# Four merge-gate half jobs placed inside the prompt attention of a hybrid decoder step, with scores three units ahead and the compressed branch in two halves

## The reference, cut to what matters

```
ng, mg = sigmoid(...)                        # from n @ w_in, w_in[:, 2328:4376] are the merge gates
p_c = softmax(q . kc)                        # compressed branch: at most 32 compressed keys
o = g[..., 0]*(p_c @ vc) + g[..., 1]*o_selected + g[..., 2]*o_window
y = (mg[:, :, 0] * y_conv + mg[:, :, 1] * (o @ w_nsa_out)) @ w_o
x += y;  x += HierMoE(RMSNorm(x));  y_out = RMSNorm_final(x)
```

## Time and profile before

| | |
|---|---|
| runs | 836.99, 840.41, 842.74 us; median 840.41 |
| profiled execution | given by its span of 835.7 us, first to last instruction; the page gives no time around it |
| PE busy | 778.5 us, 93% of the span |
| DVE, ACT, POOL busy | 375.9, 221.1 and 168.2 us |
| chain that ended last | PE 79%, DMA 9%, DVE 6%, issue 3% |
| PE on the chain, gates (L2105) | 15% of the span |
| PE on the chain, attention (L2148, L2123, L2136) | 2% each |

### The profile page before, as it was taken

One profiled execution on the slowest core, in us unless ns is written; L12 is line 12 of the kernel. 1 busy time (PEld: TensorE's weight loads), 2 busy tenths in 40 slices (PEclk: granted clock), 3 DMA queues, 4 the chain that ended last, 5 costly groups with the idle time before them and its releaser, 6 DMA issues.

```text
span 835.7 us, 11541 instructions
## 1 busy us (share of the span) xinstructions
PE 778.5 (93%) x4479; PEld 534.8 (64%) x4479; DVE 375.9 (45%) x799; ACT 221.1 (26%) x480; POOL 168.2 (20%) x270
## 2 busy tenths in 40 slices
PE   5999999997999989999999999999999899998773
PEld 3657778674756657777777777774456755555431
DVE  2201999899778881102006552231237522231106
ACT  2001324152256662233025640000001112221113
POOL 2348447010110006000004520002000212232100
PEclk9999999999999999999999999999999999999979
DMA  9775446130180005152214539703106999999737
GB/s 302 174 17 182 143 101 166 25 122 1 50 292 2 2 2 178 51 176 76 75 51 127 179 89 294 285 1 113 50 26 235 380 374 411 407 403 391 304 137 259
DMA packets 87505, 138.98 MB, mean 166 GB/s; under 512 B 25493, under 2 KB 60465, under 8 KB 86287
## 3 DMA queue, kind: packets, MB, share of 16 engines
q1 hardware_dynamic: 71439, 101.41, 35.5%
q0 software_dynamic: 11392, 32.71, 13.2%
q10 hardware_dynamic: 4616, 4.08, 1.6%
HBM read 132.00 MB, written 21.14 MB: 183 GB/s over the span
## 4 chain that ended last, share of the span: by engine, by line
PE 79%; DMA 9%; DVE 6%; issue 3%; SPq 1%; ACTq 0%; ACT 0%; DVEq 0%; POOLq 0%; POOL 0%
PE ps L1915 18%; PE ps L2105 15%; PE ps L2363 7%; PE ps L2441 6%; PE ps L1939 5%; PE ps L2012 4%; PE ps L2457 3%; DMA mgT<-w_up 2%; PE ps L2148 2%; PE ps L2123 2%; DMA arena<-w_up 2%; PE ps L2136 2%; DMA mgT<-w_in 2%; DMA arena<-yscratch 2%; PE ps L2431 1%
## 5 line engine op out<-in xcount | busy, mean ns | idle before, releaser
L2105 PE MATMUL ps<-xT,keep 128*128 128x288 f32 x512 | 126.9, 407 | 0.8 <-ACT h L1206 0.5
L2105 PEld LDWEIGHTS ps<-xT,keep 128*128 128x128 f32 x512 | 96.5, 190 | 27.4 <-ACT h L1206 0.9
L1915 PE MATMUL ps<-xT,arena 128*128 128x288 f32 x384 | 95.4, 407 | 0.0
L1915 PEld LDWEIGHTS ps<-xT,arena 128*128 128x128 f32 x384 | 72.1, 190 | 19.2
L1395 DVE SCALAR_TENSOR_TENSOR cv<-keep,cv 128x512 f32<-128x512 f32 x120 | 83.7, 748 | 1.4
L2363 PE MATMUL ps<-arena,xT 128*128 128x512 f32 x128 | 55.4, 592 | 0.0
L2441 PE MATMUL ps<-keep,mgT 128*64 128x256 f32 x224 | 41.8, 390 | 4.9 <-DMA mgT<-w_up 3.2
L1939 PE MATMUL ps<-mgT,xT 128*128 128x512 f32 (+1 forms) x128 | 43.5, 498 | 1.2 <-DMA mgT<-w_in 1.2
L2363 PEld LDWEIGHTS ps<-arena,xT 128*128 128x128 f32 x128 | 24.2, 190 | 29.3 <-issue 29.2
L836 ACT ACTIVATE mgT<-ps 64x512 f32<-64x512 f32 x56 | 33.2, 593 | 32.2 <-PE ps L1993 31.6
L1276 ACT ACTIVATE keep<-h 128x1024 f32<-128x1024 f32 (+1 forms) x5 | 5.3, 1059 | 130.1 <-DVE h L1706 121.5
(11 more groups left out here) (412 smaller groups left out, 1340.1 us busy)
## 6 DMA issues: line engine op xcount, KB each, us to landing
arena<-w_down SPq DMA_DIRECT2D x19, 512.0 KB, 16.8
keep<-w_in SPq DMA_DIRECT2D x16, 512.0 KB, 3.8
arena<-w_gate SPq DMA_DIRECT2D x15, 512.0 KB, 8.5
arena<-w_up SPq DMA_DIRECT2D x15, 512.0 KB, 12.5
keep<-w_gate SPq DMA_DIRECT2D x14, 512.0 KB, 10.4
keep<-w_up SPq DMA_DIRECT2D x14, 512.0 KB, 17.6
h<-x_prompt SPq DMA_DIRECT2D x8, 512.0 KB, 5.4
arena<-w_in SPq DMA_DIRECT2D x8, 512.0 KB, 7.5
```

The source lines that it names most:

```text
L1915: last = mm(tokens(j)[:, b, :], weights(k), halves(x[:, k, :])[:, b, :], start=k == 0, stop=k == n_k - 1)
L2105: last = mm(out[:, 0:half], wmg[n // 2 % 3][:, k, :], xT[:, k, (n % 2) * half:(n % 2 + 1) * half], start=k == 0, stop=k == KD - 1, skip_gr ...
```

## The change

- `GATES_IN = 4`: half jobs 0 to 3 of the gates go into the attention, in slot 3: half job 0 in `obank` before the first value products, half jobs 1 to 3 in `cbank`, whole or in pieces of one or two of their eight matmuls behind the value products of units 0 to 5, 12 to 17 and 19 to 23. ScalarE copies them into `mgT` without the sigmoid, which it does for the four at once after the attention.
- TensorE's order in a unit becomes `turns(u)`, `scores(u + 3)`, `values(u - 1)`, then a piece of a gate.
- The compressed branch runs for two head groups at a time: scores of 512 columns instead of 256, softmax passes twice as wide and half as many, transposes onto 128 partitions, `PcT` on all partitions, `vcB` held twice.
- The eighteen empty transposes are left out; half job 0 stands there.
- The third place of the weight ring moves to `keep3`. Tiles 0 and 1 are issued when the taps of the convolution are done, tiles 2 and 3 after the last rotated query; tiles 4 and 5 after the attention.
- After the attention, half jobs 4 to 7 stand where 0 to 3 stood, 8 to 11 where 4 to 7 stood, 12 and 13 where 8 and 9 stood, and 14 to 21 where 10 to 21 stood.

```diff
+GATES_IN = 4
+ORDER += mg_jobs(0, GATES_IN)
-ORDER += [("keys", 0, 0), ("keys", 0, 1)] + mg_jobs(0, 4) + ["mean"] + mg_jobs(4, 8) + [("keys", 0, 2)] + mg_jobs(8, 10) + ["var"] + mg_jobs(10, 22)
+ORDER += [("keys", 0, 0), ("keys", 0, 1)] + mg_jobs(GATES_IN, 8) + ["mean"] + mg_jobs(8, 12) + [("keys", 0, 2)] + mg_jobs(12, 14) + ["var"] + mg_jobs(14, 22)
...
-        wmg = [cut(1024 * s, KD, P, base=k2) for s in range(3)]
+        wmg = [cut(1024 * s, KD, P, base=k2) for s in range(2)] + [cut(2080, KD, P, base=k3)]
...
+        gate_pieces = [(0, 2), (2, 4), (4, 5), (5, 6), (6, 7), (7, 8)]
+        gates_behind = {u: (1, *gate_pieces[u]) for u in range(PER_C)}
+        gates_behind.update({2 * PER_C + n: (2, *gate_pieces[n]) for n in range(PER_C)})
+        gates_behind.update({3 * PER_C + 1 + n: (3, *x) for n, x in enumerate([(0, 2), (2, 4), (4, 5), (5, 6), (6, 8)])})
+        C_SCORES, C_LESS, C_NORM, C_TURNS = PER_C + 1, PER_C + 2, PER_C + 3, 2 * PER_C - 1
...
 # SyncE
-            conv_done(sp)
+            for c in range(CC):
+                sp.wait_ge(s_tap[c], TAPS)
             take(sp, JOB["cso"])
-            for n in range(3):
+            for n in range(2):
                 mg_weights(n)
+            result_of(sp, JOB["rope", HPG - 1])
+            mg_weights(2)
+            mg_weights(3)
             sp.wait_ge(s_kvout, 16 * N_KVOUT)
             sp.wait_ge(s_pv, NU)
             keys_window(0)
             values_window(0)
-            for n in range(3, 6):
+            for n in range(4, 6):
                 mg_weights(n)
             keys_window(1)
             sp.dma_start(wco, a["w_conv_out"][0].rearrange("(c p) n -> p c n", p=P)).then_inc(s_wo, 16)
             for n in range(6, 2 * KD):
                 mg_weights(n)
...
 # ScalarE, after the attention
             keys_turned(0, 0)
-            merge_gates(*range(4))
+            result_of(act, JOB["mg", GATES_IN - 1])
+            nc.scalar.activation(mgT[:, 0:GATES_IN // 2, :], mgT[:, 0:GATES_IN // 2, :], ACT.Sigmoid)
+            merge_gates(*range(GATES_IN, 8))
...
 # VectorE, in the attention
-                if u % PER_C == 2 and u // PER_C + 1 < HPG:
-                    cmp_maxima(u // PER_C + 1)
                 probs_turned(u)
-                if u % PER_C == 4 and u // PER_C + 1 < HPG:
-                    cmp_normalize(u // PER_C + 1)
+                if u == C_LESS:
+                    cmp_maxima(1)
+                if u == C_NORM:
+                    cmp_normalize(1)
...
 # VectorE, compressed values
-                r = slice(g * STR_P, (g + 1) * STR_P)
-                last = V.tensor_copy(vcB[r, g * HD:(g + 1) * HD], slot(j)[r, g * HD:(g + 1) * HD])
+                for n in range(2):
+                    r = slice((2 * n + g) * STR_P, (2 * n + g + 1) * STR_P)
+                    last = V.tensor_copy(vcB[r, g * HD:(g + 1) * HD], slot(j)[r, g * HD:(g + 1) * HD])
...
 # TensorE
+            def gate_columns(n, k0, k1):
+                j = JOB["mg", n]
+                if k0 == 0:
+                    if n in (1, 2):
+                        pe.wait_ge(s_cpt, n)
+                    claim(pe, j)
+                last = merge_gate(n, gate_home(n), k0, k1)
+                if k1 == KD:
+                    fill(last, j)
...
             cmp_scores(0)
             scores(0)
             scores(1)
-            for _ in range(18):
-                tr(turned[0][:, 0:P], ident[:, :], ident[:, :])
+            gate_columns(0, 0, KD)
+            scores(2)
             cmp_turns(0)
             for u in range(NU):
-                if u + 2 < NU:
-                    scores(u + 2)
-                if u % PER_C == 2 and u // PER_C + 1 < HPG:
-                    cmp_scores(u // PER_C + 1)
                 turns(u)
-                if u % PER_C == 5 and u // PER_C + 1 < HPG:
-                    cmp_turns(u // PER_C + 1)
+                if u == C_TURNS:
+                    cmp_turns(1)
+                if u + 3 < NU:
+                    scores(u + 3)
+                if u == C_SCORES:
+                    cmp_scores(1)
                 if u % PER_C == 1:
                     cmp_values(u // PER_C)
                 if u:
                     values(u - 1)
+                if u in gates_behind:
+                    gate_columns(*gates_behind[u])
...
             keys(0, 0, 1)
-            merge_gates(0, 1, 2, 3)
+            merge_gates(*range(GATES_IN, 8))
             conv_done(pe)
             over_channels(JOB["mean"], cv)
-            merge_gates(4, 5, 6, 7)
+            merge_gates(8, 9, 10, 11)
             keys(0, 2)
-            merge_gates(8, 9)
+            merge_gates(12, 13)
```

More of the change, by code:

```diff
@@ L93 @@
 for n, name in enumerate(ORDER):
-    home = n % SLOTS
+    home = 3 if J_ATT <= n < J_ATT + GATES_IN else n % SLOTS
     if n >= JOB["small", 0]:
@@ L281, in build @@
         kcB = cut(3808, 2 * STR_P, base=k3)
-        vcB = cut(3872, P, parts=2 * STR_P, base=k3)
+        vcB = cut(3872, P, base=k3)
         wdw = cut(4000, CC, TAPS, base=k3)
@@ L582, in build, with gate_home @@
         cbank, obank = ps[:, 3, 0:512], ps[:, 3, 512:1024]
-        cscores = cbank[:, 0:QT * NKV * STR_P].rearrange("p (n k) -> p n k", k=STR_P)
-        cstat = [stats[:, 16 * NU + 24 * c:16 * NU + 24 * c + 24].rearrange("p (s n) -> p s n", s=3) for c in range(HPG)]
+        cscores = cbank.rearrange("p (n k) -> p n k", k=STR_P)
+        cstat = [stats[:, 16 * NU + 48 * h:16 * NU + 48 * h + 48].rearrange("p (s n) -> p s n", s=3) for h in range(2)]
+        gate_pieces = [(0, 2), (2, 4), (4, 5), (5, 6), (6, 7), (7, 8)]
[3 more added lines that the diff above has]
+        C_SCORES, C_LESS, C_NORM, C_TURNS = PER_C + 1, PER_C + 2, PER_C + 3, 2 * PER_C - 1
+        def gate_home(n):
+            return obank if n == 0 else cbank
         @block.sync
@@ L1148, in exps, with cmp_exps, cmp_turned, gate_kept @@
                                              accum_out=x.stat(1)[:, g, b:b + 1]).then_inc(s_exp, 1)
[L1150 to L1158, removed]
+            def cmp_exps(h):
+                act.wait_ge(s_cless, h + 1)
+                nc.scalar.activation(Pc, Pc, ACT.Exp).then_inc(s_cexp, 1)
+            def cmp_turned(h):
+                act.wait_ge(s_cturn, h + 1)
+                if h:
+                    act.wait_ge(s_heads, 2 * h)
+                nc.scalar.activation(PcT, cbank, ACT.Copy).then_inc(s_cpt, 1)
+            def gate_kept(n):
+                half = T // 2
+                j = JOB["mg", n]
+                take(act, j)
+                give(nc.scalar.activation(mgT[:, n // 2, (n % 2) * half:(n % 2 + 1) * half], gate_home(n)[:, 0:half], ACT.Copy), j)
             def probs_turned(u):
@@ L1174, in _ @@
             for u in range(NU):
-                if u % PER_C == 0:
-                    cmp_turned(u // PER_C)
+                if u % (2 * PER_C) == 0:
+                    cmp_turned(u // (2 * PER_C))
+                if u in (0, 3 * PER_C):
+                    gate_kept(0 if u == 0 else 2)
                 probs_turned(u)
@@ L1212, in _ @@
             give(nc.scalar.activation(halves(rstd), tokens(j), ACT.Copy), j)
-            merge_gates(4)
+            merge_gates(8)
             for c in range(CC):
@@ L2090, in _ @@
             claim(pe, j)
-            for g in range(NKV):
-                last = mm(slot(j)[g * STR_P:(g + 1) * STR_P, g * HD:(g + 1) * HD], upper[:, g, STR_S:STR], w2[:, 1, :], start=True, stop=True)
+            for n in range(2):
+                for g in range(NKV):
+                    r = slice((2 * n + g) * STR_P, (2 * n + g + 1) * STR_P)
+                    last = mm(slot(j)[r, g * HD:(g + 1) * HD], upper[:, g, STR_S:STR], w2[:, 1, :], start=True, stop=True)
             fill(last, j)
@@ L2166, in cmp_turns @@
                 last.then_inc(s_cturn, 1)
             def cmp_values(c):
-                pe.wait_ge(s_cpt, c + 1)
+                pe.wait_ge(s_cpt, c // 2 + 1)
                 if c:
                     pe.wait_ge(s_oT, c)
-                mm(obank, vcB[:, :], PcT, start=True, stop=False, skip_group_check=True).then_inc(s_heads, 1)
+                else:
+                    result_of(pe, JOB["mg", 0])
+                r = slice(c % 2 * 2 * STR_P, (c % 2 + 1) * 2 * STR_P)
+                mm(obank, vcB[r, :], PcT[r, :], start=True, stop=False, skip_group_check=True).then_inc(s_heads, 1)
```

77 lines of the change are left out of this document (43 added, 34 removed).

## The result

| | before | changed |
|---|---|---|
| time, median of 4 runs each | 838.7 us | 851.36 us (848.71 to 852.49) |
| ratio | | 1.0159, 95% interval 1.013 to 1.0188 |
| the same comparison repeated on another chip, 7 and 4 runs | 836.58 us | 848.53 us, ratio 1.0124, 1.0075 to 1.0172 |
| profiled execution | span 835.7 us | 851.16 us, span 849.4 us |

The changed kernel is slower by about 1.2 to 1.6%. The forecast was +6.3 us within about 4 either way, and most likely within 1%; measured are +12.0 (in the repeat) and +12.7. The direction was right, but half of the loss was not in the sum. That 851.4 lies inside the range is luck: the range reached up so far only for rivals 3 and 4 (852.4 and 851.9), and neither of them happened. The profiled spans differ by 13.7 us, and the following goes by them.

The account below looks back on a forecast made before the run. TensorE was taken to bound the kernel from attention through gates. Moving gates gives -8.4 us, the wait for tile 6 +13.1, the slow clock behind it +1.6: +6.3 on 840.4, so 846.7 us, range 839 to 853.

Parts of the forecast that it names:

- Rival 3: Attention: transposes' waits for VectorE all return, 7.7 us, so idle moves instead of going; +12.0, 852.4 us; chance 0.12.
- Rival 4: Gate stage: tile 6 shares its loading with tiles 7 and 8, wait 18.3 instead of 13.1; 851.9 us; chance 0.09.
- SyncE's queue: Gate stage: TensorE waits for weight tile 6 behind the third key slot, +13.1 us, bounds 5.3 and 18.3.
- The clock behind it: Gate stage: TensorE restarts at 1.2 GHz after the wait for tile 6, +1.6 us, bounds 0 and 3.2.
- New waits: Attention: 2.0 us of new waits, VectorE's compressed work coming in lumps in units 8 and 9; bounds 0 and 7.7.
- In front of the attention: Before the attention: copies into vcB double from two to four, with two more small matmuls; +0.6 us.
- The attention: First compressed score to key transposes: 94.9 us plus 2.0 of waits, about 97; wrong if over 101 or under 94.
- 1.4 us lost: Attention: time lost at 1.2 GHz after the longest early wait, subtracted from the stage's 90.4 us to get work.
- The gates add 15.5: Attention: the four moved half jobs add 15.5 us there, the time they took in the gate stage.
- Rival 2: Attention takes all the gates without growing, argued from weight-load shares; -0.8 us, 839.6 us; chance 0.08.
- Whatever comes after the gates only shifts: Behind the gates: later stages start later but gain or lose no time; no term in the sum.

Follow-up runs that it names:

- gate0_first: Changed kernel with weight tiles 4 to 8 issued before the third key slot, plus half of half job 0 before the first compressed scores: 833.39 us, ratio 0.9962.
- tiles early: Changed kernel with SyncE issuing weight tiles 4 to 8 before its wait for the third key slot: 834.26 us, ratio 0.9971.

## Why the prediction was right in its direction and wrong in size

*SyncE's queue: right.* The need had moved past the third key slot and the load had not. The wait of 13.1 us is exactly the term of the sum, in the place and with the releaser that were named, and 13.0 in the repeat; moving the issue takes it away. The sum rested on the row of the same sequence of loads in the kernel before, where nobody waited for it; that was the better choice than either bound. Rival 4, three tiles sharing the wait (18.3), falls: tile 6 landed in 11.46 us with the others behind it.

*The clock behind it: right.* 1.7 us (9.47 against 7.76) for a forecast of 1.6; 2.8 in the repeat (10.60), inside the bounds of 0 and 3.2.

*New waits: oversized.* 0.7 instead of 2.0, one wait in unit 11 at 281.95, behind VectorE's second lump as the place was named. The scores three ahead and the gates together cover the rest (3.2 us stay without the gates). Rival 3, the idle that moves instead of going, falls with it: 0.7 of 7.7 came back.

*In front of the attention: as forecast in the wait* (+0.5 for +0.6), though in these two profiles the stage starts 0.27 us earlier, not later.

*The attention: undersized, by two steps.* The prediction took 97 us and named over 101 as wrong; the profile has 101.62 and the repeat 100.01.
The first step that failed is "1.4 us lost", taken out of the stage as though it went with the waits it stood behind. The spell came back at another place, behind a wait that the change had itself made longer, and cost about 3.4 us (1.7 in the repeat). The prediction had read the clock behind the great wait and not behind the small one.
The second is "The gates add 15.5". Three of the four half jobs, cut into 17 pieces, take 13.8 us instead of 11.6, 2.2 more than in a stream. At full clock the forecast had the stage grow by 7.9 us (-1.2 - 2.1 - 7.0 + 15.5 + 0.7 + 2.0); 2.2 more for pieces and 1.3 less for waits give 8.8, and 9.5 is measured. The missing 0.7 us don't come with the gates alone: the kernel without gates in the attention has 85.8 us where 88.7 less its transposes and waits (1.2, 2.5 and 0.6) would be 84.4. About 0.5 lie in the masks, which now have other work behind them: by start times they take 5.8 us in `gate0_first` and 5.3 before. The rest is within what these readings can tell.

*Rival 2, the attention takes all the gates without growing, falls.* It grew by 9.5 us at full clock. In the changed kernel the weight loads take 68.19 of 101.62 us, 67% and not the gate stage's 79%, while TensorE idles for only 1.5 us: the listed waits were the better measure of the room. The Trainium skill ("Trainium Kernel Development and Optimization", Performance Expectations) calls the busy share of weight loads a good measure of how near a kernel is to its roof; set against the share of another stage, with matmuls of other widths, it did not tell the room here.

*"Whatever comes after the gates only shifts": wrong, and the rest of the miss.* In the first profile the routing and the first expert bring +4.0 us by themselves, seen in the chain of the changed kernel from 640 to 690 us and of the kernel before over the same work.

```profile
648.88 20.24 issue
...
681.18 5.07 PE ps L2492 x32
```

```profile
638.61 17.72 issue
...
667.91 3.63 PE ps L2441 x32
```

"Issue" here covers the routing's small steps with empty transposes between them, at 1.2 GHz for 6.8 us of it: +2.52. The first 32 expert matmuls run partly at 1.2 GHz too: +1.44. In the repeat these two rows are back at 17.70 and 3.63, but there 2.5 us come in behind the last expert's matmuls instead (the shift is 10.5 up to them and 13.0 at the end); over the whole run it is +13.7 and +13.0. That more than a shift is at work also shows without the profile: by the same estimate as above the changed kernel's eight runs spent 49 us on average at 1.2 GHz, the kernel before 30. About 10 of the 19 more lie in the wait itself (10.7 and 8.4 in the two profiles), where they cost nothing; the 9 left cost at most half, 4.5 us, and the 1.7 to 2.8 behind the wait, for which the sum had 1.6, are among them. The kernels with the tiles early and the new order have 34 to 37 us without a stall; the first of them shows -2.4 us of the -8.4 that the forecast had for the change without the wait. By length at full clock (mean span less half of the time at 1.2 GHz, 815.1 and 820.5) it is 5.4 us shorter than before, so by estimate about 3 went into the clock (36.0 us per run against 29.6, half of the difference). Why these kernels run at 1.2 GHz longer outside the attention stays open: the spells fall at different places in two executions of the same kernel, and no run here isolates what places them.

## What to carry to other kernels

When work moves past a fixed point of an engine's program, go through every queue that issues its loads in program order and look what stands between the old and the new place of the need: the loads don't move with it, and the row of the load where nobody waited gives the price (here 13 us, five times what the rest of the change brings). Filling idle with work brings only what the idle was worth: 7.0 us of listed waits, with 3.3 us of transposes left out, took 15.5 us of gates at the price of 9.5. And a wait of 1.5 us on TensorE at the start of a stage can cost more than itself: a spell at 1.2 GHz of 3.4 us or more followed it each time. Work that is ready anyway can stand in its place and took the spell away in all three profiles, though a gain in the whole kernel's time was too small to show.

## What was unexpected in the hardware

- A spell at 1.2 GHz behind one short wait differed in length between executions of the same kernel: 6.8 and 3.4 us, 10.2 and 3.4 us, with the same 1.55 us of wait in front.
- A wait of 1.48 us between ordinary work was followed by no spell, and one of 0.57 us in front of the short compressed scores was, in one and the same profile.
- Time at 1.2 GHz, estimated from span and mean clock, differed between kernels by up to 16 us per run: 29.6 us before, 40.0 with the new order of scores and no gates, 45.7 with the gates and the old order, 34.2 in the version with whole jobs and half of the first in front.
- A run of matmuls with one accumulator that is cut into pieces between other work costs about 0.1 us for most pieces, whether they have two records or four, although TensorE's rows list no wait in between.
